# Sample states read as plain fp32 in four column groups of the tensor engine

## What is computed

```python
b = jnp.cumsum(gc, axis=2)
bL = b[:, :, -1:]
qd = qc * jnp.exp(b)
A = jnp.einsum('bhtd,bhjd->bhtj', qd, kc * jnp.exp(-b))
A = jnp.where(causal, A, 0.0)
o = jnp.einsum('bhtd,bhdv->bhtv', qd, S) + jnp.einsum('bhtj,bhjv->bhtv', A, vc)
S_new = jnp.exp(bL)[:, :, 0, :, None] * S + jnp.einsum('bhjd,bhjv->bhdv', kc * jnp.exp(bL - b), vc)
```

## Time and profile before

| | |
|---|---|
| median of 3 executions | 2125.36 us (2122.82 to 2125.43) |
| profiled execution, first to last instruction | 2122.2 us; the profile gives no time outside this span |
| busy: PE, PEld, DVE, ACT, POOL | 2039.6, 1829.8, 1307.7, 838.6, 282.9 us |
| share of the span: PE, DVE, ACT | 96%, 62%, 40% |
| mean granted clock of the tensor engine | 0.982 of full |
| this stage | from 1651.8 us to the end |

### The profile page before, as it was taken

One profiled execution on the slowest core, in us unless ns is written; L12 is line 12 of the kernel. 1 busy time (PEld: TensorE's weight loads), 2 busy tenths in 40 slices (PEclk: granted clock), 3 DMA queues, 4 the chain that ended last, 5 costly groups with the idle time before them and its releaser, 6 DMA issues. The chain is left out here.

```text
span 2122.2 us, 32885 instructions
## 1 busy us (share of the span) xinstructions
PE 2039.6 (96%) x12598; PEld 1829.8 (86%) x12598; DVE 1307.7 (62%) x2265; ACT 838.6 (40%) x1536; POOL 282.9 (13%) x430
## 2 busy tenths in 40 slices
PE   7999999999999799999969999999999699999998
PEld 7999999999999687787659999999999577777774
DVE  5466676645564767666655557667554565666663
ACT  5555543323231544444434444333221444343333
POOL 0000000000000621111100000000000653333221
PEclk9999999999999899999979999999999899999998
DMA  3121133443333654555332333343433545544442
GB/s 139 55 65 62 56 95 82 138 155 96 109 111 95 230 166 143 161 170 151 95 132 86 91 90 94 122 157 107 123 104 93 198 162 171 169 174 162 169 143 71
DMA packets 210406, 264.89 MB, mean 125 GB/s; under 512 B 49284, under 2 KB 157060, under 8 KB 208216
## 3 DMA queue, kind: packets, MB, share of 16 engines
q1 hardware_dynamic: 210264, 262.95, 39.5%
HBM read 172.91 MB, written 89.99 MB: 124 GB/s over the span
## 5 line engine op out<-in xcount | busy, mean ns | idle before, releaser
L587 DVE TENSOR_TENSOR pa_stage<-pa_ps,pa_stage 128x536 f32<-128x536 f32 x110 | 77.0, 712 | 122.6 <-PE pa_ps L554 114.4
L587 DVE TENSOR_TENSOR pc_stage<-pc_ps,pc_stage 128x536 f32<-128x536 f32 x110 | 77.0, 712 | 97.9 <-PE pc_ps L554 83.5
L401 PE MATMUL pa_ps<-a_XT_hi,pa_w_hi 128*128 128x358 f32 x576 | 133.2, 340 | 0.3 <-PEq L208 0.3
L401 PE MATMUL pa_ps<-a_XT_hi,pa_w_lo 128*128 128x358 f32 x576 | 125.9, 327 | 0.0
L401 PE MATMUL pa_ps<-a_XT_lo,pa_w_hi 128*128 128x358 f32 x576 | 125.8, 326 | 0.0
L1475 PE MATMUL mc_ps<-mc_wout_hi,mc_mix_hi 128*128 128x512 f32 x256 | 106.9, 418 | 8.7 <-POOL mc_mix_lo L3219 8.7
L554 PE MATMUL pc_ps<-c_XT_hi,pc_w_hi 128*128 128x268 f32 x384 | 110.2, 287 | 0.0
L554 PE MATMUL pa_ps<-a_XT_hi,pa_w_lo 128*128 128x268 f32 x384 | 110.1, 287 | 0.0
L554 PE MATMUL pc_ps<-c_XT_hi,pc_w_lo 128*128 128x268 f32 x384 | 110.1, 287 | 0.0
L554 PE MATMUL pc_ps<-c_XT_lo,pc_w_hi 128*128 128x268 f32 x384 | 110.1, 287 | 0.0
L554 PE MATMUL pa_ps<-a_XT_lo,pa_w_hi 128*128 128x268 f32 x384 | 110.0, 287 | 0.0
(11 more groups left out here) (588 smaller groups left out, 6114.3 us busy)
## 6 DMA issues: line engine op xcount, KB each, us to landing
pa_w_raw<-in_w_a SPq DMA_DIRECT2D x57, 512.0 KB, 4.7
pc_w_raw<-in_w_c SPq DMA_DIRECT2D x49, 512.0 KB, 4.6
scr_c<-pc_stage SPq DMA_DIRECT2D x48, 512.0 KB, 3.2
scr_a<-pa_stage SPq DMA_DIRECT2D x40, 512.0 KB, 3.2
mc_sample_state<-in_s SPq DMA_DIRECT2D x32, 512.0 KB, 4.6
out_s_s<-mc_sample_state SPq DMA_DIRECT2D x32, 512.0 KB, 2.7
ma_sample_state<-in_c SPq DMA_DIRECT2D x32, 257.0 KB, 4.1
out_c_s<-ma_sample_state SPq DMA_DIRECT2D x32, 257.0 KB, 3.2
```

What stands on the lines that cost most here:

```text
L401: ins = pe.matmul(self.ps[:, 3 * s + t, 0:TC], w[:, k, :], x[:, k, t * TC:(t + 1) * TC], start=(k == 0 and j == 0), stop=(k == KT - 1 and ...
L587: dve.tensor_tensor(dst, self.out(p, product), x, ALU.add).then_inc(self.added, 1)
```

## The change

The states are read as they arrive, in plain fp32. `csh`, `csl`, the instructions that write them and their semaphores go. `qm` holds one plain copy of q, 32 columns for each sequence. The read is four program matmuls of 32 columns by 256, one for each half d of the key width and each half j of the value width, and each has its own 32 output partitions (`quarter(2d + j)`) in the same 256 columns of bank 2, so each has a column group of the tensor engine of its own. PE waits for the state's DMA itself. The ring gets a third buffer. The scores' product at the end of a head is made in two halves, and what ACT copies and DVE adds there is made of two halves too.

```diff
-        qm = a.sb("mc_q_masked", [P, 2, NSEQ * (2 * NS + SLEN)], F32R)
-        csh, csl = (a.sb(f"mc_sample_state_{x}", [P, 2, GV], F32R) for x in ("hi", "lo"))
+        qm = a.sb("mc_q_masked", [P, 2, NSEQ * (NS + SLEN)])
...
+        HV = GV // 2
+
+        def quarter(j):
+
+            return ps[j * NS:(j + 1) * NS, 2, 0:HV]
...
-                    pe.wait_ge(cs_lo_ready, u + 1)
+                    pe.wait_ge(s_in[r], 16 * (u // SRING) + 16)
                     for d in range(2):
-                        for j, x in enumerate((csh, csl)):
-                            ins = pe.matmul(ps[0:2 * NS, 2, :], qm[:, d, 2 * b * NS:2 * (b + 1) * NS], x[:, d, :],
-                                            start=(b == 0 and d == 0 and j == 0), stop=False)
+                        for j in range(2):
+                            ins = pe.matmul(quarter(2 * d + j), qm[:, d, b * NS:(b + 1) * NS], cs[r][:, d, j * HV:(j + 1) * HV],
+                                            start=(b == 0), stop=(b == NSEQ - 1 and d == 1))
...
-                        pe.matmul(ps[0:2 * NS, 2, :], ss[g % 2][:], vT[g % 2][0:2 * NS, :].bitcast(F32), start=False, stop=True
-                                  ).then_inc(os_done, 1)
+                        for j in range(2):
+                            ins = pe.matmul(quarter(j), ss[g % 2][:], vT[g % 2][0:2 * NS, j * HV:(j + 1) * HV].bitcast(F32),
+                                            start=False, stop=True)
+                        ins.then_inc(os_done, 1)
...
-                    act.activation(gns[:], ps[NS:2 * NS, 2, :], ACT.Copy).then_inc(os_low, 1)
+                    for j in range(2):
+                        ins = act.activation(gns[:, j * HV:(j + 1) * HV], quarter(2 + j), ACT.Copy)
+                    ins.then_inc(os_low, 1)
...
-                def sample_state_hi(u):
-                    act.wait_ge(s_in[u % SRING], 16 * (u // SRING) + 16)
-                    if u:
-                        act.wait_ge(read_done, u)
-                    act.activation(csh[:], cs[u % SRING][:], ACT.Copy).then_inc(cs_hi_ready, 1)
...
-                    dve.tensor_tensor(gns[:], ps[0:NS, 2, :], gns[:], ALU.add).then_inc(os_sum, 1)
-
-                def sample_state_lo(u):
-                    dve.wait_ge(cs_hi_ready, u + 1)
-                    dve.tensor_tensor(csl[:], cs[u % SRING][:], csh[:].bitcast(F32), ALU.subtract).then_inc(cs_lo_ready, 1)
+                    for j in range(2):
+                        x = gns[:, j * HV:(j + 1) * HV]
+                        ins = dve.tensor_tensor(x, quarter(j), x, ALU.add)
+                    ins.then_inc(os_sum, 1)
...
-                        hi, lo = (qm[:, d, :].rearrange("p (s r) -> p s r", r=2 * NS + SLEN)[:, :, x:x + SLEN] for x in (0, NS))
-                        ins = masked_q(hi, lo, hs_in[0][:, d, :].rearrange("p (s t) -> p s t", t=SLEN), d + 1)
+                        ins = pool.tensor_copy(qm[:, d, :].rearrange("p (s r) -> p s r", r=NS + SLEN)[:, :, 0:SLEN],
+                                               hs_in[0][:, d, :].rearrange("p (s t) -> p s t", t=SLEN))
...
-SRING = 2
+SRING = 3
```

More of the change, by code:

```diff
@@ L2671, in stage_mix_c @@
         kw = [a.sb(f"mc_group_keys{s}", [K3, 256], F32R) for s in range(2)]
-        ss = [a.sb(f"mc_sample_scores{s}", [2 * NS, 2 * NS]) for s in range(2)]
+        ss = [a.sb(f"mc_sample_scores{s}", [2 * NS, NS]) for s in range(2)]
         gns = a.sb("mc_sample_normed", [NS, GV])
@@ L2681, in stage_mix_c @@
         r_in = sem("mc_r_in")
-        init_done = sem("mc_init_done")
         turned = sem("mc_turned")
@@ L2705, in stage_mix_c @@
         qm_ready = sem("mc_q_masked_ready")
-        qm_chain = sem("mc_q_masked_chain")
         qm_next = sem("mc_q_masked_next_ready")
-        cs_hi_ready = sem("mc_sample_state_hi_ready")
-        cs_lo_ready = sem("mc_sample_state_lo_ready")
         read_done = sem("mc_sample_read_done")
@@ L2963, in _ @@
                 first_turn(5)
-                pe.wait_ge(init_done, 2)
                 for n in range(NSTEP):
@@ L3089, in _ @@
                         copy_sample_lows(u // NSEQ)
-                    if n < UNITS:
-                        sample_state_hi(n)
                     if n + 1 < H:
@@ L3098, in _ @@
             def _(dve):
-                for x in ss:
-                    dve.memset(x[:, NS:2 * NS], 0.0).then_inc(init_done, 1)
                 def part_a(n):
@@ L3155, in scores @@
                     for i in range(2):
-                        ins = dve.tensor_tensor(ss[g % 2][i * NS:(i + 1) * NS, 0:NS], AUX[0:NS, 0:NS], mask_s[:], ALU.mult)
+                        ins = dve.tensor_tensor(ss[g % 2][i * NS:(i + 1) * NS, :], AUX[0:NS, 0:NS], mask_s[:], ALU.mult)
                     ins.then_inc(aux_read, 1)
@@ L3197, in _ @@
                         sum_samples(u // NSEQ)
-                    if n < UNITS:
-                        sample_state_lo(n)
                     if n + 1 < H:
@@ L3246, in next_q @@
                     pool.wait_ge(read_done, u + 1)
-                    hi, lo = (qm[:, :, s * (2 * NS + SLEN) + x:s * (2 * NS + SLEN) + x + SLEN] for x in (0, NS))
-                    masked_q(hi, lo, hs_in[g % 2][:, 0:2, s * SLEN:(s + 1) * SLEN], 3 + u).then_inc(qm_next, 1)
+                    pool.tensor_copy(qm[:, :, s * (NS + SLEN):s * (NS + SLEN) + SLEN],
+                                     hs_in[g % 2][:, 0:2, s * SLEN:(s + 1) * SLEN]).then_inc(qm_next, 1)
                 def stack_lo(g, j):
@@ L3264, in _ @@
                 link = linker(pool, pool_chain)
-                link(pool.memset(qm[:].bitcast(F32), 0.0))
+                link(pool.memset(qm[:], 0.0))
                 for t in range(3):
```

## The result

The changed kernel takes 2110.21 us (median of 4, 2109.22 to 2113.10) against 2124.09 us (median of 4, 2122.46 to 2125.43) in the same comparison: a ratio of 0.9941, 95% interval 0.9928 to 0.9953. By the three ratios it is faster by some 0.5%, 10 to 12 us; the two medians above lie 13.9 us apart. The direction of its sum was right and its size was not, and the rival "all at once" (2104.6 us) comes nearer. That 2110 lies in the range of 2103 to 2146 says little, as the range was drawn wide enough to hold both rivals.

The account below looks back on a forecast made before the run. PE bounds the kernel. Reads +4.4, steps 2 and 3 -3.0, first wait -2.1, small waits -0.5, scores -0.8 make -2.0 us: from 2125.4 to 2123.4 us, range 2103 to 2146.

Parts of the forecast that it names:

- The read: PE's read of each state: 1.075 us after the change, 0.145 more than now, +4.4 us over 30 units.
- The scores' product: PE's product at L2934, four times: 1.00 us falls to 0.79, together -0.8 us.
- all at once: Rival for PE's reads: all four column groups run together, 0.45 us less a read, 2104.6 us in all; chance 0.26.
- if the read is not near 1.08 us: Sign against the prediction: PE's time from the read's first record to the update's product differs from about 1.08 us.
- the stair: Chosen case for PE's reads: records start in program order, 5 slots in place of 8, 1.075 us; chance 0.42.
- the second record of a pair stands in the way unless each group can hold one record in waiting: Argument against full overlap of the four column groups in PE's read, the case put at 2104.6 us.
- The lower bound of the read: PE's read with all four groups together: starting 8 records at 0.06 us each takes 0.48 us, 0.45 less than now.
- The switches: PE's width changes, two a read, 64 in all: nothing to 0.10 us each, 0 to 6.4 us; taken as 0.
- The first wait: PE's 8.7 us wait at the start for POOL's low part of the mixed head: -2.1 us, from 0.5 to 2.6.
- Steps 2 and 3: PE's waits for late DVE in these steps: 1.4 and 1.6 us gained, -3.0 together, bounds 0 to 3.8.
- Small waits: PE's small waits in later steps, at L2947 and L2930: -0.5 us, from 0 to -1.
- The loads and the third buffer: State loads by DMA: the third buffer starts nothing earlier; cost and gain nothing, no PE wait for a DMA.

Follow-up runs that it names:

- e2: Changed kernel with the read's key halves in two column groups, value halves added: 2123.33 us in turn (A B A B), 2124.45 us in blocks (A A B B).
- e1: Changed kernel with all products of a read, and the scores', in the same 32 output partitions (one column group): 2150.41 us, ratio 1.0142 to the kernel before.
- e3: Changed kernel with each read made twice in a row into the same sums: 2124.02 us, ratio 1.0014 to the kernel before.
- e7: Changed kernel with the reads of two units made together at each even unit, loads issued a step earlier: 2103.93 us, ratio 0.9924 to the kernel before.
- e9: The kernel before, unchanged, run once more for a second profile: span 2119.0 us.
- e4: Changed kernel, but ACT's and DVE's state splits still made and unread, PE waiting for them, two buffers: 2116.8 us, ratio 0.9982 to the kernel before.
- e5: Changed kernel with two state buffers in place of three: 2111.47 us, ratio 0.9957 to the kernel before.
- e8: The changed kernel as it is, run once more beside the reads in pairs: 2112.76 us, ratio 0.9954 to the kernel before.

## Why the prediction was wrong where it was, and right where it was

**The read: wrong, and this is the step that failed.** The forecast chose "records start in the program's order, ... the second waits for the first. The next matmul's first record can run beside the second record of the one before, but not earlier": five slots, 1.075 us. It is 0.57, and by the forecast's own sign (wrong "if the read is not near 1.08 us") its mechanism failed. e2 in blocks refutes the stair, e1, e2, e3 and the changed kernel together give one rule for all four lengths:

| | records in the longest group | measured us | 0.14 + 0.215 x records |
|---|---|---|---|
| changed, four groups | 2 | 0.57 | 0.57 |
| e2, two groups, both orders | 4 | 0.99 | 1.00 |
| e3, four groups, read twice | 4 | 1.00 | 1.00 |
| e1, one group | 8 | 1.85 | 1.86 |

I had the evidence against my choice in hand, as a condition: "the second record of a pair stands in the way unless each group can hold one record in waiting". e2 in blocks shows a group with its first record running and three behind it, and the other group at work. The rows that I took the stair from held products in one column group alone, and with more groups the starts do not keep program order (e2). The rule of three groups from the Trainium skill, page "TensorE: Matmul & The Clock Gate", Part 3, pointed the right way; the runs agree with it (four groups: 1.85 / 0.57 = 3.2 with the fixed part, or 4 in slots). Its sentence that matmuls start in strict program order was no bound here, and e2 in blocks differs from it: two records have started in the first 0.24 us.

**The lower bound of the read: right in kind, mis-sized.** I took 0.48 us from the issue of eight small matmuls. e3 shows the issue to be faster than the array; what stands instead is 2 slots and a fixed 0.14 us, 0.57. It also left out the 0.19 of switches, so "all at once" came out too fast by 0.28 us a read.

**The switches: wrong value, right bound.** I took 0 of 0 to 0.10 each, after a row with a read of 64 columns. With 32 columns it is 0.09 in and 0.10 out, 0.19 a read, some 6 us in all; e7 takes half of them out, and the time goes with them. The row to go by was the earlier trace rows, where the 0.10 stood ahead of another change of width. The Trainium skill, page "TensorEngine Tiling (Array Packing)", Key Properties, says that a change of tiling mode drains the engine; it gives no price. The 0.19 us agrees with it, and that nothing shows around the old read, with its 64 columns, does not follow from it.

What the cost hangs on can be read in the kernel before, in its first layer. Four transposes of 32 columns (L1939, one record each) stand there between products of 128, and a plain fp32 product of 32 columns (L1948, the samples' scores of that layer):

```profile
771.37 0.41 PE L1927 MATMUL ma_ps<-ma_sample_v_stack,ma_group_keys 96*128 96x258 f32 x2
771.62 0.60 PE L1939 MATMUL ma_ps<-ident,ma_sample_in 128*32 128x128 f32 x4
771.98 0.48 PE L1475 MATMUL ma_ps<-ma_wout_hi,ma_mix_hi 128*128 128x512 f32 x1
...
801.82 0.40 PE L1927 MATMUL ma_ps<-ma_sample_v_stack,ma_group_keys 96*128 96x258 f32 x2
802.15 0.62 PE L1948 MATMUL ma_ps<-ma_sample_v_stack,ma_sample_scores 64*32 64x257 f32 x2
802.69 0.50 PE L1475 MATMUL ma_ps<-ma_wout_hi,ma_mix_hi 128*128 128x512 f32 x1
```

The two records of L1927 take 0.12 us each. The transposes begin 0.25 us after them, so nothing is paid; the plain product begins 0.33 us after, 0.08 to 0.09 more. So 32 columns alone don't cost it. Nor does plain fp32 alone: at L2879, with 128 columns, the first record starts 0.11 us behind the last transpose before it, as the transposes do behind each other. Nor does the number of groups, as e1 has the same 0.32 us into its read. Narrow and plain together had the gap ahead of them in the three places looked at: L1948, L2934 and the new read. L1948 also had the price of two records in one group in it, 802.69 - 802.15 = 0.54 us, with the fixed part beside 2 x 0.215. The forecast used neither.

The two errors had opposite signs: 0.36 us off a read in place of 0.145 on it, and 0.19 of switches on it in place of none. Net 0.17 less a read, where the forecast had 0.145 more: over 30 reads 5.1 us gained in place of 4.4 lost, 9.5 of the 13.2 us between the forecast and the first result. The scores' product is another 1.0, and the kernel before ran 1.3 us faster in that comparison than the median which the sum was made against. The rest is the comparison's own scatter: the start and the steps 2 and 3 gained 1.2 us less than forecast, and the traces hold 11.2 us where the first two medians have 13.9.

**The first wait: right.** Predicted -2.1, and it is 6.6 in place of 8.7. In parts, by the time from the stage's start to the release: 25.45 us before (e9), 24.30 in e4, 23.44 changed. The shorter POOL work gives 1.15 (forecast 1.1), DVE's missing low part 0.86 (forecast 1.0). e4 shows how: the eight pieces take 7.56 us there too, but POOL's state scale behind them takes 3.02 in place of 2.04. In both traces with the splits POOL loses 3 us in all, and which of its instructions lose it depends on what runs then. That it is DVE's split and not ACT's that costs POOL the last 1.0 us is argued from the times; e4 has both. Only 1.42 of the 2.0 us reach the first read. In e9 the matmuls after the wait run at 1.2 GHz for 3.6 us before they rise to 2.4, in the changed kernel for 4.5 us; in the first profile of before it was 6 us. PE's stretch at the low clock behind a wait is work to be counted with the wait.

**Steps 2 and 3: near.** Predicted -3.0 at their ends. The intervals from the second to the fourth read go from 12.72 + 14.30 to 11.42 + 13.08, -2.5 us. The wait for `mc_state` went as said; that for `mc_scores_lo` was to fall under 0.3 us and is still 0.69 in step 2, and 0.67 in step 3. DVE's order of time shows the rest of its lateness, a weight split behind ACT's copy:

```profile
1687.97 2.60 DVE L1438 TENSOR_TENSOR mc_wout_lo<-wout_c_early,mc_wout_hi 128x1024 fp32r<-128x1024 f32 x2 [1.65 <-ACT mc_wout_hi L1428]
...
1692.75 0.64 DVE L3108 TENSOR_TENSOR mc_scores_lo<-mc_scores,mc_scores_hi 128x128 fp32r<-128x128 f32 x1
```

**Small waits: right.** Three intervals between reads go from 12.55 to 12.20, of which 0.17 is the read: 3 x 0.18 = 0.5 us. **The scores' product:** -0.44 each, by the group rule again (forecast -0.2). **The loads and the third buffer: right**, by e5.

**By the rule now known**, the forecast's own sum would be 30 x -0.17 - 3.0 - 2.1 - 0.5 - 1.8 = -12.5 us, against -11.2 in the traces of e8 and e9 and -10 to -12.5 by the three ratios.

What is open: what the fixed 0.14 us of a read is made of, and why narrow plain products pay on the way in and out and narrow transposes don't. The last stretch of the table gained 0.36 us though its read and its scores' product give 0.7: 0.3 of this goes back where PE waits 0.6 us for DVE's low part of the values (L3111) in place of 0.3 (L3118). Why the clock falls near the end in some executions was not tried.

## What to carry to other kernels

Narrow plain-fp32 products spread over four column groups cost by the longest group's list, so give each group the same number of records and don't mind their order; then put such products together, for each change between them and the 128-wide products was paid anew here. Before a cost is said to have no row, look for the new shape in the other stages of the same trace. Before a term of the sum is charged with "this must wait for that", ask whether the waiter stands in the common queue or in one of its own, and keep both prices. And take a second profile of the kernel before when the granted clock dips in a stretch that the sum covers.

## What the runs showed of the hardware that was not expected

- Column groups work through their records independently: A A B B is as fast as A B A B, 0.99 us for eight records of 256 columns in plain fp32, and group B's first record starts while three of group A's, ahead of it in the program, still wait.
- A change between 128-wide products and plain fp32 reads of 32 columns cost 0.09 us in and 0.10 out, plus 0.14 us once a block of such reads; in e7 a pair of steps with one block less is 0.37 us shorter. For the fp32r reads of 64 columns, for transposes of 32 and for plain fp32 of 128 columns nothing showed on the way in.
- POOL's slowdown beside the splits came to the same sum in two traces: 3.0 us too much in 8 pieces (8.50 for 5.56, e9), or 2.0 in the pieces and 1.0 in the two instructions behind them (e4).
- Spells at 1.2 GHz of some 3.5 us appear near the end of some executions of the same kernel and not of others, 1.6 us each.
